# A LayerNorm between two chains of products: the mean taken by a product with ones, and one scaling step a tile in place of two

## What is computed

```python
def layer_norm(x, g, b, eps=1e-5):
    xf = x.astype(jnp.float32)
    mu = jnp.mean(xf, -1, keepdims=True)
    var = jnp.mean(jnp.square(xf - mu), -1, keepdims=True)
    return ((xf - mu) * lax.rsqrt(var + eps)).astype(x.dtype) * g + b

    x = layer_norm(x, ln_in_g, ln_in_b)                  # norm 1
    for l in range(2):
        ...
        x = layer_norm(DN_ALPHA * x + (1.0 + g1) * (ym @ w_out[l]), ln1_g[l], ln1_b[l])   # norms 2 and 4
        ...
        x = layer_norm(DN_ALPHA * x + (1.0 + g2) * conv_ffn(...), ln2_g[l], ln2_b[l])     # norms 3 and 5
```

## Time and profile before

| | |
|---|---|
| median of 3 runs | 1342.56 us (1342.15 to 1351.18) |
| the profiled execution | 1341.11 us |
| its span in the trace | 1339.3 us |
| TensorE busy | 97% of the span |
| VectorE, ScalarE, GpSimd busy | 67%, 40%, 18% |
| mean granted clock of TensorE | 0.98 |

### The profile page before, as it was taken

The page is one execution under the profiler, slowest core; times in us unless marked ns, Lnnn a source line. Parts: engine busy times, 40 slices in busy tenths (PEclk is TensorE's granted clock), DMA queues, the critical chain, the costliest instruction groups (busy, mean ns, idle before and its releaser), DMA issues.

```text
span 1339.3 us, 17200 instructions
## 1 busy us (share of the span) xinstructions
PE 1293.7 (97%) x6802; PEld 1000.5 (75%) x6802; DVE 901.0 (67%) x1537; ACT 532.4 (40%) x796; POOL 242.4 (18%) x201
## 2 busy tenths in 40 slices
PE   6899999999999999999899999999999999999997
PEld 3445776786888888888766677778688888888886
DVE  5986878676877777768656857676765555563335
ACT  2524225335533334434227543443463333343323
POOL 0640102445000000000039331153420000000003
PEclk9999999999999999999989999999999999999998
DMA  9454644021666666755217151122123332223321
GB/s 388 176 141 136 158 150 129 17 97 60 221 192 199 190 191 189 268 191 184 80 52 202 53 110 33 48 79 79 63 95 97 104 98 95 95 95 96 97 91 63
DMA packets 65232, 170.90 MB, mean 128 GB/s; under 512 B 14336, under 2 KB 27008, under 8 KB 64256
## 3 DMA queue, kind: packets, MB, share of 16 engines
q1 hardware_dynamic: 65152, 169.81, 39.9%
HBM read 162.07 MB, written 7.72 MB: 127 GB/s over the span
## 4 chain that ended last, share of the span: by engine, by line
PE 83%; DVE 12%; DMA 1%; issue 1%; POOL 1%; ACT 1%; SPq 0%; ACTq 0%; POOLq 0%
PE bank L565 21%; PE bank L566 20%; PE bank L567 20%; PE bank L688 3%; PE bank L682 2%; PE bank L715 2%; PE bank L580 2%; PE bank L585 1%; PE bank L843 1%; PE bank L880 1%; PE bank L574 1%; PE bank L1153 1%; DVE scr L1855 1%; DVE xa L1292 1%; PE bank L852 1%
## 5 line engine op out<-in xcount | busy, mean ns | idle before, releaser
L565 PE MATMUL bank<-ym_r,scr_r 128*128 128x512 f32 x688 | 268.8, 391 | 4.8 <-DVE hm_r L1960 2.5
L567 PE MATMUL bank<-hm_r,scr_r 128*128 128x512 f32 x688 | 267.9, 389 | 0.0
L566 PE MATMUL bank<-ym_r,ring_r 128*128 128x512 f32 x688 | 267.8, 389 | 0.0
L1361 DVE TENSOR_TENSOR ring_r<-ring,scr_r 128x1024 fp32r<-128x1024 f32 x134 | 165.6, 1236 | 86.3 <-ACT scr_r L2131 86.1
L2131 ACT ACTIVATE scr_r<-ring 128x1024 fp32r<-128x1024 f32 x146 | 153.4, 1052 | 128.0 <-DMA ring<-in_w_down 105.6
L565 PE MATMUL bank<-scr_r 128*128 128x512 f32 x480 | 190.1, 396 | 6.0 <-DVE scr_r L1986 3.8
L566 PE MATMUL bank<-scr_r,ring_r 128*128 128x512 f32 x480 | 188.5, 393 | 0.0
L565 PEld LDWEIGHTS bank<-ym_r,scr_r 128*128 128x128 f32 x688 | 129.1, 188 | 36.5 <-issue 6.2
L567 PEld LDWEIGHTS bank<-hm_r,scr_r 128*128 128x128 f32 x688 | 129.1, 188 | 27.0
L566 PEld LDWEIGHTS bank<-ym_r,ring_r 128*128 128x128 f32 x688 | 129.2, 188 | 26.3
L2474 ACT ACTIVATE scr<-bank,pb 128x512 f32<-128x512 f32 x86 | 67.0, 779 | 194.0 <-PE bank L567 194.0
(11 more groups left out here) (396 smaller groups left out, 2027.9 us busy)
## 6 DMA issues: line engine op xcount, KB each, us to landing
ring<-in_w_up SPq DMA_DIRECT2D x88, 512.0 KB, 3.6
ada<-in_w_ada SPq DMA_DIRECT2D x80, 512.0 KB, 3.6
ring<-in_w_down SPq DMA_DIRECT2D x44, 512.0 KB, 3.5
ring<-in_w_in SPq DMA_DIRECT2D x33, 512.0 KB, 4.3
scr<-in_w_ada SPq DMA_DIRECT2D x16, 512.0 KB, 14.0
ring<-in_w_out SPq DMA_DIRECT2D x16, 512.0 KB, 3.6
pa<-in_par_a SPq DMA_DIRECT2D x2, 2144.5 KB, 12.9
xa<-in_x SPq DMA_DIRECT2D x1, 2048.0 KB, 8.0
```

The source lines that it names most:

```text
L565: first = mm(dst, w_hi, x_hi, start=start, stop=False)
L566: mm(dst, w_lo, x_hi, start=False, stop=False)
L567: return first, mm(dst, w_hi, x_lo, start=False, stop=stop)
L1361: V.tensor_tensor(ring_r[:, slot(l, n), :], ring[:, slot(l, n), :], high[:, slot(l, n), :].bitcast(F32), ALU.subtract)\
```

## The change

For norms 2 to 5 (norm 1 keeps the old way as `first_stats` and `first_apply`):

- `sum_x` adds all eight tiles, and `sums_spread` multiplies `acc[:, 0]` with a matrix of ones, 512 columns, so that every partition of a bank holds the sum over all channels. The group of one-column products on the last tile of `xa` goes, that on the last tile of `hm` stays.
- VectorE makes `hm = xa - sum / 1024` out of place, eight SCALAR_TENSOR_TENSOR instructions (`centre`, L1319 of the new kernel): four before `norm_var`, three between it and the reciprocal, the last behind the reciprocal. Mean times reciprocal is no longer made.
- Only the reciprocal deviation is spread (`rstd_spread`, four products of 128 columns, once; twice in norm 5), and one multiplication a tile (`xa = hm * factor`, L1339) ends the norm.
- `collect` moves from behind the reciprocal into the residual loop, behind the sum of tile 6 and ahead of that tile's `weights_low`.
- The correction of the raw chunk changes its order (subtract, then multiply). In norm 5 GpSimd has one multiplication a tile in place of two steps, and ScalarE copies one bank in place of two. There PE takes the squares' sum first.

```diff
+            def sums_spread(n, bank):
+                pe.wait_ge(S["ln_sumx"], n)
+                mm(banks[bank][:, :], ones, acc[:, 0, :], start=True, stop=True).then_inc(S["ln_bcast"], 1)
+
+            def norm_stats(n, late, first):
+                norm_sums(acc[:, 0, :], 64, first, True)
+                if first:
+                    pe.wait_ge(S["ln_sumq"], n)
+                    norm_sums(acc[:, 1, :], 68, False, False)
+                pe.wait_ge(S["ln_sq"], n * KD)
+                norm_sums(hm[:, late, :], 68, False, True).then_inc(S["ln_stat"], 1)
...
+            def rstd_spread(n, bank):
+                pe.wait_ge(S["ln_rstd"], (n - 1) * 2 + 1)
+                for b in range(NB):
+                    last = spread(banks[bank][:, b * P:(b + 1) * P], 12 + b, P)
+                last.then_inc(S["ln_bcast"], 1)
...
                 raw_slice(1)
-                norm_stats(2 * l + 2, KD - 1)
+                sums_spread(2 * l + 2, 0)
+                norm_stats(2 * l + 2, KD - 1, True)
                 raw_slice(2)
                 raw_slice(3)
                 raw_slice(4)
-                norm_spread(2 * l + 2)
+                rstd_spread(2 * l + 2, 1)
...
-                    norm_pause(2 * l + 3, DOWN_DONE[-1])
+                    pe.wait_ge(S["ln_sumq"], 2 * l + 3)
+                    norm_sums(acc[:, 1, :], 68, True, False)
+                    sums_spread(2 * l + 3, 0)
+                    norm_stats(2 * l + 3, DOWN_DONE[-1], False)
+                    keep_awake(1)
+                    rstd_spread(2 * l + 3, 1)
+                    rstd_spread(2 * l + 3, 3)
...
+            def norm(n, order, low=None):
...
+                    return V.scalar_tensor_tensor(hm[:, k, :], sums[:, :], -1.0 / D, xa[:, k, :], ALU.mult, ALU.add)
                 v.wait_ge(S["ln_bcast"], (n - 1) * 2 + 1)
+                v.wait_ge(S["ln_sumq"], n)
+                for k in order[:4]:
+                    ch.post(centre(k))
+                norm_var(n)
+                for k in order[4:KD - 1]:
+                    ch.post(centre(k))
+                v.wait_ge(S["ln_sd"], n)
+                V.reciprocal(rstd, var).then_inc(S["ln_rstd"], 1)
+                centre(order[KD - 1]).then_inc(S["ln_rstd"], 1)
+                ch.settle()
+                v.wait_ge(S["ln_rstd"], n * 2)
+                v.wait_ge(S["ln_bcast"], (n - 1) * 2 + 2)
+                for k in range(KD - SHARED if last else KD):
...
+                    V.tensor_tensor(xa[:, k, :], hm[:, k, :], factor[:, :], ALU.mult).then_inc(S["ln_normed"], 1)
+                    if low is not None and k >= 2 and k % 2 == 0:
+                        low(k - 2)
```

114 lines of the change are left out of this document (47 added, 67 removed).

## The result

The changed kernel takes 1336.37 us, the median of 9 runs (1331.62 to 1341.26). The kernel before, in as many runs beside it, takes 1346.30 (1342.15 to 1351.18). The ratio is 0.9927, with a 95% interval from 0.9902 to 0.9952: 9.8 us less, between 6.5 and 13.2, and inside the 1% that the prediction took for no change. The forecast was 1337.4 us, in a range from 1332.5 to 1342.0, and 5.2 us less than before. In three later sessions the kernel before gave medians of 1342.88 to 1343.68, so some of the 9.8 us is a high median of before; against 1342.56 the gain is 6.2 us.

A forecast was written before the change was run, and what follows sets the result against it. TensorE, busy 97% of the span, was taken as the bound. Norms 2 and 4 at -2.0 us each, norm 3 -2.4 and norm 5 +1.2 make -5.2, from 1342.56 to 1337.4 us; range 1332.5 to 1342.0.

The forecast's parts named there:

- Statistics "cost nothing" in norms 2 and 4: Norms 2 and 4: one narrow group (0.87 us) goes, one wide product (0.86) comes, the sum arriving in time: no cost.
- The fold: Moved `collect`, norms 2 and 4: residual of tile 7 between 0 and 0.67 us late, taken as 0.6; the move gains nothing.
- The reciprocal, norms 2 and 4: Reciprocal 2.0 us later, hidden by TensorE's slices if the clock falls as before; first multiplication then +0.6 us.
- One step a tile: Norms 2 and 4: GpSimd starts low parts 3.1 to 3.5 us after the first multiplication; 1.7 or 2.6 us gained, taken as 2.0.
- the branch with the clock held: Norms 2 and 4 at full clock: TensorE waits 0.9 us for the reciprocal, and GpSimd's list is 2.6 us earlier.
- Norm 3: Norm 3: -0.9 us if half clock lasts as long as before, -3.5 if the clock holds; taken as -2.4.
- Between the norms TensorE's list is unchanged and full, so what a norm gives stays.: Stretches between the norms: no change in length, so the total is the sum of the norms, -5.2 us.
- Norm 5: Norm 5: nothing covers `centre`, TensorE idles some 3.3 us; +1.3 or -0.4 us, taken as +1.2.
- The clock holds: Rival, chance 0.25: 2.4 GHz through the narrow products in all four norms, norm 5 too; -9.1 us, 1333.5 us.
- GpSimd eats the gain: Rival, chance 0.18: faster VectorE collides more with GpSimd, leaving little gain in norms 2 to 4; -1.0 us, 1341.6 us.
- the slower rival: Chance 0.05: each `centre` takes 1.1 us rather than 0.68, delaying the reciprocal 2.9 us in four norms; +11.8, 1349 us.
- Nothing comes out: Rival, chance 0.07: something behind the norms, such as a weight transfer, was nearly as late; 1342.5 us.

The follow-up runs named there:

- The two experiments: Changed kernel with the reciprocal directly behind the variance, ahead of the remaining four `centre`: 1336.76 us; changed kernel with two unread products added in norm 5: 1335.57 us.

## Why the prediction was right, point by point

- **The time.** 1336.37 us for 1337.4, near the middle of the range. The change against before is larger than forecast (6.5 to 13.2 less, for 5.2), so a part of the agreement is the median from which I started. A larger part is luck. In the profile the norms gave 5.0 us for 5.2 only because their errors cancel: norms 2 and 4 gave 1.4 each for 2.0, norm 3 3.9 for 2.4, norm 5 cost 1.6 for 1.2. And another 4.0 us came from stretches to which I had given nothing.
- **Statistics "cost nothing" in norms 2 and 4.** Mis-sized by 0.8 us: 6.00 for 5.20. The wide product takes 0.96, the group that goes 0.7, and the sum is 0.53 late (939.92, where two slices of 0.86 end at 939.39), after a residual that is 0.5 us late.
- **The fold.** I took the residual 0.6 us late, and it is 0.5 us. The end of the norm moved by 0.34 with it. The step that said the old place hides it is right (the kernel before with the fold alone moved: no change), the mechanism (a collision with GpSimd's sum) shown in the rows above.
- **The reciprocal, norms 2 and 4.** Right: hidden by three slices at half clock, first multiplication +0.68 for +0.6. The kernel with the reciprocal first shows that the three `centre` cost nothing there. The other branch, that with the clock held TensorE would wait 0.9 for it, came true in the kernel with the products spread out: 0.96.
- **One step a tile.** GpSimd's first low part 3.54 after the first multiplication, the upper end of 3.1 to 3.5. So 5.61 - 3.54 - 0.68 = 1.39 us, which is what the norm gave. The forecast of 2.0 lay too near the branch with the clock held, and the sign that I had named (L565 1.5 to 2.5 us closer to raw slice 0) was just missed, at 1.38.
- **Norm 3.** Both ends were as worked out: -0.9 with equal half clock (14.44 to 13.51), -3.5 with the clock held, measured 12.20 for 16.12, which is -3.9. In a given execution it is the one or the other; a value in between was a mean of two cases. What makes the clock hold or fall there stays open: the same instructions gave both in different kernels. Norm 3 alone, with what follows it in layer 2, carries the most of the gain (-5.2 us).
- **"Between the norms TensorE's list is unchanged and full, so what a norm gives stays."** This step failed, on the good side. VectorE and GpSimd ended norm 3 some 3 us earlier, GpSimd's unbroken list in layer 2 moved with it, and VectorE's chain, for which TensorE waits 56 us into the layer, met less of it. TensorE's product behind that wait came 2.7 us earlier (58.90 to 56.22 after the first L880). The earlier trace rows hide such a wait, as 97% busy leaves 45.6 us of gaps in the span. I had named what would show me wrong, a stretch far from the norms that changes its length: by that sign the prediction is wrong here, though its number held. That GpSimd's list is the cause is read from the rows, as said above. The other 1.0 us of the pair's 3.7 goes with half clock (10.2 us for 13.6, and another place).
- **Norm 5.** +1.6 for +1.2. The reciprocal came 7.7 us after GpSimd's sum, as worked out, but by errors that nearly cancel: `centre` took 0.62 us and not 0.68, and VectorE waited 0.66 us for statistics that TensorE made at half clock. For the same reason the TensorE gap of 3.3 us that I had named as a sign is 0.88 us (the row at 1317.90); with the clock held up to there, in the kernel with norms 2 and 4 old, it is 2.53. The spreads took the long way (1317.90 to 1321.72, at half clock). What I had not priced is that the clock falls for longer. The two experiments give 1.5 us to the order of `centre` and 2.5 to the clock, and with either alone norm 5 is shorter than it was before (17.11 and 16.62 for 17.46).
- **The rivals.** "The clock holds" came true in norm 3 and nowhere else of the changed kernel. "GpSimd eats the gain" did not: its modulated tiles took 0.90 (2.70 for three). `centre` took 0.62 a piece, not 1.1 (2.48 for four), which settles the slower rival. "Nothing comes out" is excluded by the interval.

## What to carry over

A step saved on the small engines is worth following past the edit, even where TensorE is 97% busy: as the rows read here, an unbroken list moves as a whole, and what it no longer runs beside gets shorter far away. A total that comes out right says little where its terms do not. Before a longer wait is called the proof of a cause, lay the trace beside a kernel that has the same stage without it. Slack can be spent once: two moves that cost nothing or gain 0.3 us alone cost 0.4 to 0.6 us together, while narrow products put between wide ones gave 1.1 us in each of norms 2 and 4 with nothing saved, and cost 0.9 in norm 3.
